# Hybrid encoder trunk: the gate steps of mixer A's phases in five clumps instead of seven

## The reference

```
h = rms_norm(x, g_mix)
qa, ka, va, qb, kb, vb, gate_logits = split(h @ w_in)
# A: 8 heads of 64, chunks of 64 tokens, own chunk and 8 before it
sc = qa @ ka^T / 8 + bias(relative distance)
y_a = (softmax(sc) @ va) @ w_branch_a
# B: 8 query heads, 2 key heads, rotary q and k, 128 keys, sinks
y_b = attention_b(qb, kb, vb, sinks) @ w_branch_b
g_a, g_b = split(sigmoid(gate_logits + b_gate))
x = x + (g_a * y_a + g_b * y_b) @ w_out
x = x + (silu(h2 @ w_g) * (h2 @ w_u)) @ w_down        # h2 = rms_norm(x, g_ffn)
```

## Time and profile before

| | |
|---|---|
| median of 3 runs | 2605.28 us (2604.1 to 2605.75) |
| profiled execution, its own time | 2606.36 us |
| its span in the profile | 2604.6 us |
| TensorE busy | 2571.5 us (99%) |
| VectorE, ScalarE, GpSimd busy | 1823.6, 1043.9, 283.0 us |
| granted TensorE clock, mean | 0.997 |

### The profile page before, as it was taken

One profiled execution on the slowest core, in us unless ns is written; L12 is line 12 of the kernel. 1 busy time (PEld: TensorE's weight loads), 2 busy tenths in 40 slices (PEclk: granted clock), 3 DMA queues, 4 the chain that ended last, 5 costly groups with the idle time before them and its releaser, 6 DMA issues. The chain is left out here.

```text
span 2604.6 us, 35587 instructions
## 1 busy us (share of the span) xinstructions
PE 2571.5 (99%) x12822; PEld 2095.8 (80%) x12822; DVE 1823.6 (70%) x3321; ACT 1043.9 (40%) x2071; POOL 283.0 (11%) x442
## 2 busy tenths in 40 slices
PE   8999999999999999999999999999999999999998
PEld 6888777788888888888878887778888888888886
DVE  8766555644888777768996664555458778776687
ACT  6222455532533333344642225564235333333444
POOL 0000232344000000000000002224440000000000
PEclk9999999999999999999999999999999999999999
DMA  4323543353132233385423344424422233225843
GB/s 141 132 105 112 174 131 118 127 178 127 60 117 100 91 113 114 98 278 166 154 101 120 108 145 149 140 88 161 159 110 82 89 113 121 82 105 164 261 118 125
DMA packets 200333, 336.93 MB, mean 129 GB/s; under 512 B 18672, under 2 KB 79968, under 8 KB 200160
## 3 DMA queue, kind: packets, MB, share of 16 engines
q1 hardware_dynamic: 191936, 311.47, 36.4%
q10 hardware_dynamic: 8224, 23.20, 2.6%
HBM read 240.76 MB, written 92.92 MB: 128 GB/s over the span
## 5 line engine op out<-in xcount | busy, mean ns | idle before, releaser
L1396 PE MATMUL ps<-op_hi,up_hi 128*128 128x512 f32 x1232 | 479.8, 389 | 2.5 <-DVE third_sum L2971 2.5
L1398 PE MATMUL ps<-op_hi,up_lo 128*128 128x512 f32 x1232 | 479.3, 389 | 0.0
L1397 PE MATMUL ps<-op_lo,up_hi 128*128 128x512 f32 x1232 | 479.3, 389 | 0.0
L1396 PE MATMUL ps<-in_hi,up_hi 128*128 128x512 f32 x728 | 285.7, 392 | 3.1 <-DVE up_lo L2469 2.3
L1397 PE MATMUL ps<-in_lo,up_hi 128*128 128x512 f32 x728 | 284.0, 390 | 0.0
L1398 PE MATMUL ps<-in_hi,up_lo 128*128 128x512 f32 x728 | 284.0, 390 | 0.0
L1396 PEld LDWEIGHTS ps<-op_hi,up_hi 128*128 128x128 f32 x1232 | 231.2, 188 | 51.2 <-issue 3.3
L1398 PEld LDWEIGHTS ps<-op_hi,up_lo 128*128 128x128 f32 x1232 | 231.2, 188 | 48.0
L1397 PEld LDWEIGHTS ps<-op_lo,up_hi 128*128 128x128 f32 x1232 | 231.3, 188 | 47.9
L2069 ACT ACTIVATE up_hi<-up_raw 128x512 fp32r<-128x512 f32 x252 | 158.1, 630 | 278.5 <-PE ps L1398 271.6
L1396 PE MATMUL ps<-act_hi,dn_hi 128*128 128x512 f32 x616 | 240.4, 390 | 1.2 <-DVE dn_lo L3146 1.2
(11 more groups left out here) (253 smaller groups left out, 4811.7 us busy)
## 6 DMA issues: line engine op xcount, KB each, us to landing
up_raw<-w_gu SPq DMA_DIRECT2D x42, 1024.0 KB, 5.0
act_raw<-ff_saved SPq DMA_DIRECT2D x154, 256.0 KB, 2.8
w_quarter<-w_lin SPq DMA_DIRECT2D x52, 512.0 KB, 4.5
w_raw<-w_lin SPq DMA_DIRECT2D x48, 512.0 KB, 4.3
ff_saved<-ff_block SPq DMA_DIRECT2D x88, 256.0 KB, 2.0
ff_saved<-ff_mix SPq DMA_DIRECT2D x66, 256.0 KB, 2.0
gated<-gates_saved SPq DMA_DIRECT2D x32, 512.0 KB, 4.1
dn<-w_dn_a SPq DMA_DIRECT2D x48, 256.0 KB, 4.0
```

The source lines that it names most:

```text
L1396: pe.matmul(out, w1, x1, start=first, stop=False, skip_group_check=True)
L1397: pe.matmul(out, w1, x0, start=False, stop=False, skip_group_check=True)
L1398: return pe.matmul(out, w0, x1, start=False, stop=last, skip_group_check=True)
```

## The change

The row of numbers for the runs of an A phase is altered; the sums per phase stay 24 and 10 gate steps, and the B phases keep theirs.

```diff
-FILL_A = ((8, 4, 4, 2, 2, 2, 2, 0),) + ((2, 2, 2, 1, 1, 1, 1, 0),) * (GROUPS - 1)
+FILL_A = ((8, 4, 4, 0, 4, 0, 4, 0),) + ((2, 2, 2, 0, 2, 0, 2, 0),) * (GROUPS - 1)
 FILL_B = ((4, 4, 3, 3),) * (GROUPS - 1) + ((2, 2, 2, 2),)
```

## The result

| | before | after |
|---|---|---|
| median of all runs | 2604.45 us (2603.37 to 2605.75, 8 runs) | 2612.18 us (2610.31 to 2614.52, 8 runs) |
| profiled execution: time, span | 2606.36, 2604.6 us | 2610.31, 2608.5 us |
| TensorE busy | 2571.5 us | 2568.9 us |
| stage from the first gate step to the first branch product, layer 0 / layer 1 | 220.03 / 220.16 us | 223.26 / 223.32 us |

By the medians the change makes the kernel 7.7 us slower. The ratio on record is 1.0027 of the time before, 95% interval 1.0018 to 1.0037, which is 7.0 us (4.7 to 9.6). Forecast were 6.7 us and 2612.0. The page of the kernel after: first its span, then busy time by engine, then the granted clock in 40 slices.

The account below looks back on a forecast made before the run. TensorE, busy 2571.5 of 2604.6 us, was taken to bound the kernel, so its added waits count: 4.2 + 1.3 + 1.2 = 6.7 us slower, 2605.28 to 2612.0 us. The 8-in-10 range was 2609.3 to 2614.5.

Parts of the forecast that it names:

- r3 to r4 in g1 to g3, six by 0.70: Attention, both layers: r4's scores already wait for VectorE's read, so each moved gate step is lost in full; 4.2 us.
- r3 to r4 in g0, 0.64: Attention, first group: two gate steps leave, 1.39 us, scores start only 0.75 earlier; 1.3 us over two layers.
- r5 to r6, eight by 0.15: Attention, all eight phases: a 0.70 us gate step leaves, scores start 0.56 earlier; 1.2 us, bounds 0 to 2.2.
- The pair of rows that the prediction quoted for the lock: r5 of g3: VectorE's rotary step 0.50 us longer, overlapping GpSimd's 0.73 us instruction; read as agreeing with an exclusive lock.
- The exponentials have 0.9 us of room; r4 and r6 do not lose: r5's transposes wait for ScalarE's exponentials with 0.9 us to spare; runs receiving gate steps gain more cover; no loss.
- Rival, a clump has a price: Each clump of gate steps costs about 0.18 us; 16 fewer save 2.9, giving 2609.1 us; chance 0.14.
- Rival, VectorE catches up: TensorE's wait at r4 is given back later; half back would make 2608.6 us; chance 0.04.
- Rival, the clock falls: New TensorE gaps of 1.02 us lower the clock at the four longest, adding 6.8 us: 2618.8 us; chance 0.04.
- The wait from which the prediction took its price: Early-program TensorE wait of 1.92 us, followed by granted clock 0.72 over six microseconds; priced at 1.7 us per fall.

Follow-up runs that it names:

- e4a: Changed kernel, plus VectorE issuing the rotary work of a run's first head behind the read of the second head; 2604.82 us, ratio to before 0.9996.
- e2: Kernel before, with only r5's gate steps moved behind r6, r3 and r4 keeping theirs; 2606.47 us, ratio 1.0005.
- e5: Kernel before, with r6's gate step moved ahead to r5 in g1, g2 and g3; 2604.96 us, ratio 1.0000.
- e4b: Kernel before, with VectorE issuing the rotary work of a run's first head behind the read of the second head; 2603.97 us, ratio 0.9994.

## Why the prediction was right

The forecast of 6.7 us stands against 7.7 and 6.4 measured in two batches and 6.4 in the trace. That the median came within 0.2 us of 2612.0 is in part luck: over 8 executions the kernel before has 2604.45, 0.8 under the 2605.28 from which the forecast started, and the difference came out 1.0 above the forecast. The terms are better judged in the trace.

- *r3 to r4 in g1 to g3, six by 0.70.* Right: 0.69 to 0.70 in layer 0 and 0.68 to 0.71 in layer 1; the read's end sets r4's scores in every phase, and e4a shows it by removing the rotary work from between the reads. One reading was short of the cause: the prediction took L2746's 0.91 us for the step's own time, and some 0.2 of them are the hold by GpSimd's instruction. As both kernels have it, no term changes.
- *r3 to r4 in g0, 0.64.* Measured 0.60. The read was met exactly (3.31 us); the two steps added to r4 cost 1.35 instead of 1.39. In r6 of g0, too, the third and fourth step of the clump cost 1.34. So r5 and r6 of g0 lost 0.10 instead of 0.15. This is most of the difference between 6.7 and 6.4, the rest is the rounding of 0.695 to 0.70.
- *r5 to r6, eight by 0.15.* Right in all phases but g0's, at 0.14 to 0.15, and in g3 for the reason given: the step moved behind GpSimd's instruction. e2, where nothing ahead of r5 is longer, has the overlap and its price of 0.44 us back. The pair of rows that the prediction quoted for the lock, 0.50 us extra against GpSimd's 0.73, would fit a shared port as well. What tells them apart is the end: at all 154 places in the nine profiles where such a rotary step began 0.03 to 0.53 us after a GpSimd instruction that was not held itself (0.72 to 0.76 us long), it ended 0.54 to 0.55 us after GpSimd's end, wherever it had begun. The exclusive lock of the Trainium skill (SBUF — State Buffer, section SBUF: two separate sides) fits this.
- *The exponentials have 0.9 us of room; r4 and r6 do not lose.* Nothing in the profile after contradicts it: r4 and r6 have no wait of their own.
- *Rival, a clump has a price.* It fell: e5 took six clumps away where nothing waits, for 0.00 us. The 0.3 us at either side of a clump are no extra. In r6 of g1 of the kernel before, the clump's second matmul starts 0.31 us behind the first, but the first only 0.14 behind the start of the last row of transposes. From that row to the scores of r7 it is 1.01 us with the gate step (364.58 to 365.59) and 0.32 without one in e5 (362.30 to 362.62). The difference, 0.69, is one gate step.
- *Rival, VectorE catches up.* It fell: the runs of the A phases grew by 3.2 us in each layer and the stages by 3.23 and 3.16, so B's phases gave nothing back that counts. The piece between the two stages is 0.2 us shorter in the first profile after and 0.03 in the second.
- *Rival, the clock falls.* It fell: with gaps of 1.01 us in g1 and g3 the granted clock stayed full. The Trainium skill's rule on short idles (TensorE: Matmul & The Clock Gate, section A second HAM failure mode: psum-queue depth-cycling) did not show at these gaps. The wait from which the prediction took its price doesn't lower the clock each time either: in the profile after it is as long as before, 1.93 us against 1.92, and the granted clock stays at 1.00 over 40 to 60 us.

```profile
41.48 1.26 PE L1421 MATMUL ps<-ident,x_sb 128*128 128x128 f32 x8 [1.93 <-ACT ps L1867]
```

- What I had not foreseen is the size of the spread outside the stage: the profile after lay 1.9 us under its median.

## What to carry to other kernels

Filling work in the list of a busy engine is free to move only within runs whose next wait is already met: look for the wait at the start of the next run, compare it with the end of what it waits for, and where the two are a constant few hundredths of a microsecond apart, whatever filling is taken from there is lost in full. Number and size of clumps did not matter here; their place against the late engine did. And before moving the filling, ask whether the late engine's list can be put in a better order: one reordering on VectorE made up for the whole loss (6.8 us by the stages), and with it the choice of clumps was worth 1.4 us instead of 6.4.

## What the runs showed of the hardware

- From the end of VectorE's read to the start of the matmul that waited for it: 0.05 to 0.06 us at every place read, with or without a long wait.
- A bracket of idle time understates a wait behind matmuls by 0.07 to 0.08 us: in g1 before it was 0.32, while r3 was 0.39 longer than the same work without a wait (3.53 against 3.14 in e4b); in g2 none was printed, and r3 was 0.17 longer (3.31 against 3.14).
- A rotary step of VectorE with two SBUF inputs takes 0.64 to 0.69 us by itself. Where it began 0.03 to 0.53 us after a GpSimd instruction of 0.72 to 0.76 us, it took up to 1.25 and ended 0.54 to 0.55 us after GpSimd's end, however early it had begun.
- From one execution to the next of the changed kernel, the eight small matmuls near the end took 1.16 us at a granted clock of 1.00 or 2.07 at 0.50, and the stretch from 40 to 60 us had a granted clock of 1.00 or 0.91, with a wait of 1.9 us ahead of its work both times.
